# Modulation weights in the residual's place, a new order of projections, the router on unnormalised tokens, and the first gather ahead of later weights

## The chip, the cores and the metric

One core of a Trainium2 chip runs the whole kernel in one launch. Its engines are TensorE (PE; its weight loads are listed apart as PEld), VectorE (DVE), ScalarE (ACT) and GpSimd (POOL); SyncE (SP) only issues transfers. The metric is the device time of one execution in microseconds. A change of 0.2% (1.9 us) or more can be told from none for this kernel.

## The reference

One layer of a diffusion backbone in float32, width 1024, for 512 latent tokens (4 tiles of 128) and 128 context tokens (tile 4). Each kind has its own modulation vector.

```python
mod = silu(c) @ w_mod + b_mod                      # shift1, scale1, gate1, shift2, scale2, gate2
h = rmsnorm(x, g_norm1) * (1 + scale1) + shift1
p = h @ w_in        # xb, xc, xv (512 each), q, k (256 each), v, og (512 each), a_low (32)
y_a = xb * (conv3(xc * xv) + b_conv)               # along grid rows of 64, or the context
la = log_sigmoid(a_low @ w_a_up + b_a) / 16        # decay per direction, 4 heads
y_b = per_head_rmsnorm(gla_bidirectional(q, k, v, la)) * silu(og)
x = x + gate1 * (concat(y_a, y_b) @ w_out)
h = rmsnorm(x, g_norm2) * (1 + scale2) + shift2
probs = softmax(h @ w_router)                      # 16 experts; each takes its top 64 latent
gates, idx = top_k(probs.T, cap)                   # and top 16 context tokens
x = x + gate2 * scatter_add(gates * (silu(xs @ w_gate) * (xs @ w_up)) @ w_down)
y = rmsnorm(x, g_final)
```

The outputs are y for both kinds of tokens and the two final scan states of the context.

## The kernel before

The kernel has two phases. Phase one runs everything up to the choice of tokens, in an order written out by hand for each engine; phase two loops over 16 experts.

**Phase one.** TensorE's work is a list of jobs (`first_phase_jobs`, line 101). Each job ends with one step of the semaphore `job_done`, and each writes one of four pairs of PSUM banks. `place_jobs` gives a job the pair whose last job ended longest ago, except where `FORCED` names one; before a job TensorE waits in `claim` until the pair's previous job has been read (`read_by`). `HELD` keeps a pair until a later job, `LATE` lists jobs whose order of claims differs from that of their ends. The large projections work on two roundings: a weight part and a token part are split into a high half (ScalarE, `split_hi`, line 716; tokens `tokens_hi`) and a low half (VectorE, `split_lo`, line 1118), and each product is three passes, high-high, high-low, low-high (`passes`, line 1671). The modulated tokens stand in `hT`; their low half is written over them. The low-rank product for the decays (`low_rank`, line 1691) uses full float32 matmuls on the high and the low half, one after the other. A float32 matmul shows as two records, one of the rounded form as one.

Jobs have short names: `mod5` is the product with 512 columns of `w_mod`, `modT5` its turn to columns (`mod_turn`), after which VectorE's `modulation(5)` adds the bias; `xc0` to `xc3` are four parts of a projection (`project`), `v0` to `v4` the values by token tile (`values`), `la0` a head's log-decay, `ks0` a head's turned keys, `kv` key-value products, `att`, `o`, `oT` attention, head outputs and their turn, `g1` and `g2` rows of the gates, `wo0` to `wo4` the output projection by token tile, `x2T` the turned tile for the router, `lg` the router's product, `pT` and `pTc` turned scores, `ixT`, `ixTc`, `pcT` turned choices.

Weights of phase one come in units of 2 MB. `UNITS` is the order in which SyncE asks for them (`load_unit`, line 432), `PLACES` the buffer of each; a unit waits until the previous unit of its buffer has been used. SyncE handles its list strictly in order, so a wait in it holds back everything behind. Modulation units share buffers 0 and 1 with the projections' weights. The two cached states and later the residual `x_sb` are loaded into the region at `A_X`, which holds the input tokens until they are normalised.

**Output projection and router.** `output_projection(t, half)` (line 1887) makes 512 columns of tile t: 8 rows of 3 matmuls. VectorE's loop over tiles (from line 1418) reads each half from PSUM, multiplies by gate1, adds the residual, waits for the root of the mean square from ScalarE (`second_norm`), forms the inverse (`inverse_of`, four short steps) and writes normalised rows `xr` (`normalise`). ScalarE stores these rows to `hn` and the residual to `sum_l` in memory (`store_rows`, line 928). TensorE turns the normalised rows (`x2T`), ScalarE and VectorE copy four chunks each with scale2 and shift2 applied (`h2_turn`, `high_chunks`), and `router(t)` multiplies by `w_router_sb`. After the fourth tile VectorE takes the softmax and finds the top 64 for each expert in eight rounds. The context tile goes through GpSimd (line 587) meanwhile. In TensorE's order the dummy matmuls (`keep_warm`), the wait for the normalised context rows and their turn stand ahead of the turn of the latent choice (`turn_indices("ixT", 1)`).

**Phase two.** The first gather (`gather_first`, line 602) fetches 64 latent rows from `hn`. ScalarE modulates the turned rows, and each expert runs gate and up products for latent (line 2023) and context rows (2040), then down products (2063, 2072). Two turns for gate2's rows stand within expert 0. Expert weights pass through a ring of nine 2 MB slots, six loads per expert. Loads 0 to 2 are issued when the last head is gated; loads 3 to 8 each wait for a named event, load 9 and on for their slot.

## Time and profile before

| | us |
|---|---|
| time, median of 3 runs (935.05 to 936.36) | 935.1 |
| the profiled execution's own time | 934.86 |
| its span | 933.1 |
| TensorE busy | 876.1 |
| VectorE busy | 286.6 |
| ScalarE busy | 229.1 |
| GpSimd busy | 86.2 |
| moved between memory and the core | 273.33 MB, mean 293 GB/s |

Phase one lasts until 373.8 us, when the first expert matmul starts. The page's strip of forty slices shows TensorE busy nearly everywhere but in the first and last slices and near 350 to 375 us. A row of the chain of waits is a start, a length and what ran; a row of a timeline is a start, a length, the engine, the line and operation with its operands, and in brackets how long the engine had been idle and who released it. "Issue" is time without a visible wait.

### The profile page before, as it was taken

Reading aid. Unit: us, or ns where it says so; the run is one execution under the profiler, and the core shown is the slowest. Engines: PE = TensorE matmul, PEld = TensorE weight load, DVE = VectorE, ACT = ScalarE, POOL = GpSimd, SP = SyncE. Lnnn points to the kernel's source line nnn. Section 1 sums busy time; section 2 is a strip of 40 time slices with the busy share of each in tenths; the row PEclk is TensorE's granted clock in tenths of the full one; section 3 lists DMA queues with packets and bytes.
Section 4 is the critical chain, followed back from the end, with each engine's and each line's share of the span. In section 5 each row is a group of like instructions: output and inputs, shape, how many; then the busy total and the mean of one; then the engine's idle time right before and its main releaser. Section 6 shows DMA issues by size and latency. Waiting matters only on the chain.

```text
span 933.1 us, 14292 instructions
## 1 busy us (share of the span) xinstructions
PE 876.1 (94%) x6267; PEld 494.4 (53%) x6267; DVE 286.6 (31%) x589; ACT 229.1 (25%) x449; POOL 86.2 (9%) x87
## 2 busy tenths in 40 slices
PE   5798999999999995999999999999999999999994
PEld 4587889889897885333333333333333333333331
DVE  3455443668545645211011011101101101101215
ACT  5457343453224322211011011101101101101132
POOL 1000000000000012110110110011011011011013
PEclk9899999999999998999999999999999999999997
DMA  8914454552329239699999999999999999999973
GB/s 325 308 38 164 143 176 152 190 182 91 103 113 359 105 130 370 212 354 392 380 389 402 380 380 409 380 378 403 385 379 395 394 379 389 400 381 392 410 280 126
DMA packets 86180, 273.33 MB, mean 293 GB/s; under 512 B 6068, under 2 KB 9112, under 8 KB 86120
## 3 DMA queue, kind: packets, MB, share of 16 engines
q1 hardware_dynamic: 78376, 255.15, 71.3%
q0 software_dynamic: 6128, 11.87, 5.6%
q10 hardware_dynamic: 1616, 5.42, 1.5%
q8 instruction: 49, 0.80, 0.4%
q14 instruction: 11, 0.09, 0.0%
HBM read 257.94 MB, written 14.55 MB: 292 GB/s over the span
## 4 chain that ended last, share of the span: by engine, by line
PE 80%; DMA 7%; DVE 5%; ACT 4%; issue 2%; SPq 1%; POOL 1%; POOLq 0%; ACTq 0%; DVEq 0%
PE pair L2023 24%; PE pair L2040 12%; PE pair L1686 12%; PE pair L2063 11%; PE pair L2072 6%; PE pair L1897 5%; DMA p1w<-in_w_mod 4%; DMA p1w<-in_w_in 2%; PE pair L1722 2%; PE pair L1650 2%; DVE aT L1546 1%; DVE act_c L1544 1%; DMA p1w<-in_w_out 1%; ACT act_c L1009 1%; PE pair L1910 1%
## 5 line engine op out<-in xcount | busy, mean ns | idle before, releaser
L2023 PE MATMUL pair<-ring,xT 128*64 128x512 f32 x1024 | 225.3, 596 | 0.2 <-ACT xT L983 0.2
L2023 PEld LDWEIGHTS pair<-ring,xT 128*64 128x64 f32 x1024 | 72.2, 137 | 142.4 <-issue 142.3
L2063 PE MATMUL pair<-ring,aT 128*64 128x512 f32 x512 | 113.4, 595 | 1.1
L2040 PE MATMUL pair<-ring,xT 128*32 128x512 f32 x1024 | 113.2, 594 | 0.9 <-DVE xT L1533 0.9
L1005 ACT ACTIVATE act_l<-pair 128x512 f32<-128x512 f32 x16 | 9.6, 597 | 347.9 <-PE pair L2023 347.9
L1686 PE MATMUL pair<-hT_hi,w_hi 128*128 128x320 f32 x320 | 75.7, 318 | 5.8 <-DVE w_lo L1126 5.8
L1542 DVE TENSOR_TENSOR act_l<-act_l,pair 128x512 f32<-128x512 f32 x16 | 11.0, 687 | 207.8 <-ACT act_l L1005 207.8
L2040 PEld LDWEIGHTS pair<-ring,xT 128*32 128x32 f32 x1024 | 32.0, 110 | 79.7 <-issue 79.7
L1686 PE MATMUL pair<-hT_hi,w_lo 128*128 128x320 f32 x320 | 73.5, 311 | 0.0
L1686 PE MATMUL pair<-hT_lo,w_hi 128*128 128x320 f32 x320 | 73.4, 311 | 0.0
L2063 PEld LDWEIGHTS pair<-ring,aT 128*64 128x64 f32 x512 | 35.3, 137 | 68.8 <-issue 64.0
L625 POOL DMA_INDIRECT sum_l<-y_l,row_l x15 | 23.5, 1569 | 403.8 <-DVE y_l L1537 403.8
L1686 PEld LDWEIGHTS pair<-hT_hi,w_hi 128*128 128x128 f32 x320 | 53.5, 190 | 12.5 <-issue 11.6
L2072 PE MATMUL pair<-ring,aTc 128*32 128x256 f32 x1024 | 58.9, 381 | 0.0
L1686 PEld LDWEIGHTS pair<-hT_lo,w_hi 128*128 128x128 f32 x320 | 54.0, 189 | 0.0
L1686 PEld LDWEIGHTS pair<-hT_hi,w_lo 128*128 128x128 f32 x320 | 54.0, 190 | 0.0
L2072 PEld LDWEIGHTS pair<-ring,aTc 128*32 128x32 f32 x1024 | 31.5, 110 | 32.1 <-issue 13.0
L1544 DVE TENSOR_TENSOR act_c<-act_c,pair 64x512 f32<-64x512 f32 x16 | 11.0, 690 | 102.2 <-ACT act_c L1009 102.2
L1126 DVE TENSOR_TENSOR w_lo<-p1w,w_hi 128x1024 fp32r<-128x1024 f32 x24 | 29.0, 1223 | 42.0 <-ACT w_hi L726 41.8
L991 ACT ACTIVATE xT<-pair,mod,scale 128x64 f32<-128x64 f32 x120 | 37.1, 415 | 7.9 <-PE pair L1982 7.9
L1537 DVE SCALAR_TENSOR_TENSOR y_l<-pair,gain,gate_l 128x512 f32<-128x512 f32 x16 | 12.0, 750 | 74.8 <-PE pair L2063 74.8
L1897 PE MATMUL pair<-wo_hi,yT_hi 128*128 128x512 f32 x80 | 32.3, 404 | 1.4 <-DVE yT_lo L1360 1.4
(283 smaller groups left out, 972.4 us busy)
## 6 DMA issues: line engine op xcount, KB each, us to landing
...
```

Of the source, the lines that this page charges most:

```text
L625: g.indirect_dma_start(rows_l, bass.IndirectOffsetOnAxis(ap=row_l[:, e:e + 1], axis=0), y_l[:, e % 2, :], None, compute_op=ALU.add).then_i ...
L991: ins = a.activation(xT[:, k % 2, kk, 0:CAP_L], xT_ps(kk)[:, 0:CAP_L], ACT.Identity, bias=mod[:, 3 * KC + kk, 0:1], scale=scale2[:, kk, 0:1])
L1126: v.tensor_tensor(w_lo[place][:, :, tile(j)], p1w[place][:, :, tile(j)], rounded(name)[:, :, tile(j)].bitcast(F32), ALU.subtract).then_inc ...
L1544: v.tensor_tensor(act_c[0:64, :], act_c[64:P, :], ctx_ps[64:P, :], ALU.mult).then_inc(act_c_ready, 1)
L1650: ins = mm(pp[g:g + 32, 0:512], silu_c[:, k, :], w[:, k, :], start=k < 4, stop=k >= 4)
L1686: ins = mm(pp[:, s * 512:s * 512 + HALF], w, h[:, s * HALF:(s + 1) * HALF], start=k == 0 and i == 0, stop=k == KC - 1 and i == 2)
L1722: ins = mm(pp[:, cols], h, w, start=k == 0 and i == 0, stop=k == KC - 1 and i == 2)
L1897: ins = mm(pp[:, half * 512:(half + 1) * 512], y, w, start=k == 0 and i == 0, stop=k == KC - 1 and i == 2)
L2023: ins = mm(ps[64 * n:64 * n + 64, :], xt[:, kk, 0:CAP_L], w[:, j, n * 512:(n + 1) * 512], start=kk == 0, stop=kk == KC - 1)
L2040: ins = mm(ctx_ps[32 * g:32 * g + 32, :], xt[:, kk, CAP_L:96], w[:, j, n * 512:(n + 1) * 512], start=kk == 0, stop=kk == KC - 1)
L2063: ins = mm(y_ps[0][r:r + 64, :], aT[:, j, 64 * fh:64 * fh + 64], wd[:, j, n * 512:(n + 1) * 512], start=fh == 0 and j == 0, stop=fh == 1 a ...
L2072: ins = mm(y_ps[1][32 * b:32 * b + 32, 0:256], aTc[:, j, 32 * fh:32 * fh + 32], down[fh][:, j, 256 * b:256 * b + 256], start=fh == 0 and j ...
```

## The change

It has five parts.

1. A seventh buffer for phase-one weights, `p1w6`, lies at `A_X`. Five modulation units go through it (4, 5, 10, 6 and 11; 9, 7 and 8 keep buffers 0 and 1), and `UNITS` has a new order. The states are loaded after `mod11` has been used. `wo1` is asked for ahead of the residual.
2. The tokens before splitting move from `hT` to two buffers `raw`, which aren't overwritten, so `low_rank` reads them in one float32 pass.
3. The orders of jobs change on all engines: `la1` behind `v1`, `mod5` ahead of the key turns, `mod8` behind the attention products, `xb3` ahead of `o3`, `oT4` behind the first half of `wo0`, and others.
4. The router works on unnormalised tokens. `x2T` turns `x_sb`; the copies no longer modulate; the router's weights are scaled once by scale2 (`w_scaled`); the product of shift2 with the router is made once (`rb`), copied by VectorE (`shifted`), spread over 128 rows on TensorE (`rbT`), and added when VectorE reads the logits, together with the factor 1/rms. Normalised rows are still made, for `hn`.
5. At the end of phase one gate2's rows are turned directly after the context's output projection, there are fewer dummy matmuls, load 5 of the ring waits for the first gather's landing, and ScalarE issues the copies of the context's residual to `sum_c` after `first_tokens`; load 7 waits for them as before.

```diff
+    jobs += ["mod1", "mod3", "modT1", "modT3", "q0", "q1", "k0", "alow", "k1", "la0"]
+    jobs += ["v0", "v1", "la1", "mod4", "v2", "mod9", "v3", "v4", "mod5", "ks0", "ks1", "modT4", "modT9", "la2"]
+    jobs += ["xc0", "xc1", "modT5", "xc2", "mod10", "xc3", "ks2", "modT10"]
+    jobs += ["xv0", "la3", "xv1", "mod6", "xv2", "modT6", "xv3", "mod11", "ks3"]
+    jobs += ["og0", "modT11", "mod7", "kv0", "kv1", "og1", "kv2", "kv3", "og2", "modT7", "kv4", "og3"]
+    jobs += ["xb0", "att0", "att1", "mod8", "xb1", "modT8", "o0", "att2", "o1", "oT0", "att3", "xb2"]
+    jobs += ["oT1", "o2", "att4", "xb3", "o3", "oT2", "o4", "oT3", "g1_0", "g1_1", "rb", "oT4"]
+    jobs += ["rbT", "wo0", "wo1", "x2T0", "x2T1", "lg0", "wo2", "lg1", "x2T2", "wo3", "lg2", "x2T3", "lg3", "pT", "wo4", "g2_0", "g2_1", "x2T4", "ixT", "lg4", "pTc", "ixTc", "pcT"]
...
-LATE = ["wo0", "wo1", "wo2", "x2T0", "lg0", "x2T1", "wo3", "lg1", "x2T2", "wo4", "x2T3", "lg2", "lg3", "pT"]
-HELD = {"q0": "modT3", "q1": "modT3", "k0": "modT3", "wo4": "pT"}
-FORCED = {"x2T4": 1, "ixT": 0, "lg4": 3, "pTc": 1, "ixTc": 3, "pcT": 1, "g2_0": 3, "g2_1": 1}
+LATE = ["wo0", "oT4", "rbT", "wo1", "x2T0", "wo2", "x2T1", "lg0", "lg1", "wo3", "x2T2", "lg2", "wo4", "x2T3", "lg3", "pT"]
+HELD = {"q0": "modT3", "q1": "modT3", "k0": "modT3", "mod5": "la2", "wo4": "pT"}
+FORCED = {"g2_0": 2, "g2_1": 1, "x2T4": 2, "ixT": 0, "lg4": 3, "pTc": 1, "ixTc": 3, "pcT": 1}
...
-UNITS = ["mod0", "mod2", "qk", "mod1", "mod3", "v", "mod4", "mod9", "xc", "mod5", "mod10", "xv", "mod6", "mod11", "og",
+UNITS = ["mod0", "mod2", "qk", "mod1", "mod3", "v", "mod4", "mod9", "mod5", "xc", "xv", "mod10", "mod6", "og", "mod11",
  "mod7", "xb", "mod8", "wo0", "wo1"]
-PLACES = [2, 5, 0, 1, 4, 1, 0, 0, 0, 1, 1, 1, 0, 0, 0, 1, 1, 0, 0, 1]
+PLACES = [2, 5, 0, 1, 4, 1, 6, 0, 6, 0, 1, 6, 6, 0, 6, 1, 1, 0, 0, 1]
...
+p1w.append(at("p1w6", A_X, [P, KC, 512]))
...
+w_scaled = at("w_scaled", R_V + 4096, [P, KC, 2, E])
...
-    for n in range(UNITS.index("v"), UNITS.index("og")):
-        load_unit(n)
+    load_unit(UNITS.index("v"))
     sp.wait_ge(ss_ready, NT)
     sp.wait_ge(xr_ready, NT)
+    for n in range(UNITS.index("mod4"), UNITS.index("xb")):
+        load_unit(n)
+    sp.wait_ge(job_done, job("mod11") + 1)
     sp.dma_start(states[0:DK, 0, :, :], s_fwd[0, 0].rearrange("h d v -> d h v")).then_inc(st_in, 16)
     sp.dma_start(states[DK:P, NCH_LAT - 1, :, :], s_bwd[0, 0].rearrange("h d v -> d h v")).then_inc(st_in, 16)
-    for n in range(UNITS.index("og"), UNITS.index("wo1")):
+    for n in range(UNITS.index("xb"), UNITS.index("wo1")):
         load_unit(n)
     sp.wait_ge(fin_state, 1)
     sp.dma_start(new_f[0, 0].rearrange("h d v -> d h v"), final_state[0:DK, :, :]).then_inc(state_out, 16)
     sp.dma_start(new_b[0, 0].rearrange("h d v -> d h v"), final_state[DK:P, :, :]).then_inc(state_out, 16)
+    load_unit(UNITS.index("wo1"))
     sp.wait_ge(job_done, job("o4") + 1)
     for t in range(NT):
         src = x_sample[0, tile(t), :] if t < NT - 1 else x_prompt[0]
         sp.dma_start(x_sb[:, t, :], src).then_inc(x_in[t], 16)
-    load_unit(UNITS.index("wo1"))
...
     load_rows(3)
     sp.wait_ge(job_done, job("wo4") + 1)
     load_rows(4)
+    sp.wait_ge(xs_full[0], 16)
     load_rows(5)
...
     split_hi("wo0", 0)
...
     o_square(0)
     o_square(1)
     split_hi("wo0", 2)
-    for t in range(2, NT):
-        o_square(t)
+    o_square(2)
     split_hi("wo0", 3)
+    o_square(3)
     mixed_hi(0)
     mixed_hi(1)
+    o_square(4)
     gate_row("g1_0", 0, gate1b, g1_ready)
     gate_row("g1_1", 1, gate1b, g1_ready)
...
+        rows = slice(KC // 2 * half, KC // 2 * half + KC // 2)
+        a.activation(h2T[t % 2][:, rows, :], pp[:, 512 * half:512 * half + 512].rearrange("p (k n) -> p k n", n=P),
+                     ACT.Copy).then_inc((h2_low, h2_high)[half], 1)
     for t in range(NT - 1):
-        if 1 <= t < NT - 2:
-            h2_turn(t - 1)
+        second_norm(t)
         if t + 2 < NT:
             mixed_hi(t + 2)
-        second_norm(t)
-        if t == NT - 2:
-            h2_turn(t - 1)
         store_rows(t)
-    h2_turn(NT - 2)
+        h2_turn(t)
...
     ctx_half(0)
     ctx_half(1)
+    for v in range(2):
+        gate_row(f"g2_{v}", v, gate2b, g2_ready)
     act.wait_ge(x2c_ready, 2)
     square_sum(NT - 1)
+    h2_turn(NT - 1)
+    h2_turn(NT - 1, 1)
     act.wait_ge(rootc_ready, 1)
     a.activation(xr[:, 0, :], x_sb[:, NT - 1, :], ACT.Copy, scale=rms[:, 5, NT - 1:NT]).then_inc(xrc_ready, 1)
-    h2_turn(NT - 1)
-    h2_turn(NT - 1, 1)
+    act.wait_ge(xrc_ready, 1)
     act.dma_start(hn[tile(NT - 1), :], xr[:, 0, :]).then_inc(hn_out[0], 16)
-    act.dma_start(sum_c[0:P, :], x_sb[:, NT - 1, :]).then_inc(sums_in, 16)
-    act.dma_start(sum_c[P:P + PAD, :], x_sb[0:PAD, NT - 1, :]).then_inc(sums_in, 16)
...
     first_tokens()
-    for v in range(2):
-        gate_row(f"g2_{v}", v, gate2b, g2_ready)
+    act.dma_start(sum_c[0:P, :], x_sb[:, NT - 1, :]).then_inc(sums_in, 16)
+    act.dma_start(sum_c[P:P + PAD, :], x_sb[0:PAD, NT - 1, :]).then_inc(sums_in, 16)
...
     split_lo("wo0", 2)
+    head_norm(2)
     att_mask(4)
-    head_norm(2)
+    gated_conv(3)
+    split_lo("wo0", 3)
     gated(2)
     head_norm(3)
+    mixed_lo(0)
+    mixed_lo(1)
     gated(3)
     head_norm(4)
-    gated_conv(3)
-    split_lo("wo0", 3)
-    mixed_lo(0)
     gated(4)
-    mixed_lo(1)
     for j in range(4):
         split_lo("wo1", j)
     dve.wait_ge(g1_ready, 2)
+    dve.wait_ge(job_done, job("oT4") + 1)
+    dve.wait_ge(scale_ready, 3)
+    dve.wait_ge(decay_in, 144)
+    for i in range(2):
+        ins = v.tensor_tensor(w_scaled[:, :, i, :], w_router_sb[:, :, :],
+                              scale2[:, :, i:i + 1].to_broadcast([P, KC, E]), ALU.mult)
+    ins.then_inc(wscaled_ready, 1)
+    pp = result(dve, "rb")
+    v.tensor_copy(shifted[:, :], pp[0:2, 0:E]).then_inc(rb_ready, 1)
     def high_chunks(t):
         pp = result(dve, f"x2T{t}")
         if t >= 2:
             dve.wait_ge(job_done, job(f"lg{t - 2}") + 1)
-        for k in range(KC // 2, KC):
-            ins = v.tensor_scalar(h2T[t % 2][:, k, :], pp[:, k * P:(k + 1) * P],
-                                  scale2[:, k, vec(t):vec(t) + 1], mod[:, 3 * KC + k, vec(t):vec(t) + 1],
-                                  ALU.mult, ALU.add)
-        ins.then_inc(h2_high, 1)
+        v.tensor_copy(h2T[t % 2][:, KC // 2:, :], pp[:, 512:1024].rearrange("p (k n) -> p k n", n=P)
+                      ).then_inc(h2_high, 1)
     def router_row(t):
         pp = result(dve, f"lg{t}")
-        v.tensor_copy(logits[:, t, :], pp[:, 0:E]).then_inc(lg_ready, 1)
-    dve.wait_ge(scale_ready, 3)
+        v.scalar_tensor_tensor(out=logits[:, t, :], in0=pp[:, 0:E], scalar=rms[:, 5, t:t + 1],
+                               in1=shift_rows[:, vec(t), :], op0=ALU.mult, op1=ALU.add).then_inc(lg_ready, 1)
     for t in range(NT - 1):
+        pp = pairs[PAIR[f"wo{t}"]]
+        dve.wait_ge(x_in[t], 32)
         if t >= 2:
             dve.wait_ge(hn_out[t % 2], 16 * (t // 2))
-            dve.wait_ge(job_done, job(f"x2T{t - 2}") + 1)
-        pp = pairs[PAIR[f"wo{t}"]]
-        dve.wait_ge(x_in[t], 32)
         for half in range(2):
             cols = slice(512 * half, 512 * half + 512)
             dve.wait_ge(*((wo_half, t + 1) if half == 0 else (job_done, job(f"wo{t}") + 1)))
...
                             ).then_inc(wo_read, 1)
             dve.wait_ge(wo_read, 2 * t + half + 1)
             v.tensor_tensor(x_sb[:, t, cols], x_sb[:, t, cols], xr[:, t % 2, cols], ALU.add).then_inc(x2_ready, 1)
-        if 1 <= t < NT - 1:
-            high_chunks(t - 1)
+        if t == 0:
+            pp = result(dve, "rbT")
+            v.tensor_copy(shift_rows[:, :, :], pp[:, 0:2 * E].rearrange("p (v e) -> p v e", v=2)
+                          ).then_inc(rbT_ready, 1)
         if t + 2 < NT:
             mixed_lo(t + 2)
+        if t == NT - 2:
+            high_chunks(t)
         dve.wait_ge(root_ready, t + 2)
         inverse_of(rms, slice(t, t + 1), EPS)
         normalise(t)
-        if t >= 2:
-            router_row(t - 2)
-    high_chunks(NT - 2)
-    router_row(NT - 3)
+        if t < NT - 2:
+            high_chunks(t)
+        if t:
+            router_row(t - 1)
     router_row(NT - 2)
     def softmax(lo, hi, turn):
...
+    def turn_tile(t):
+        pe.wait_ge(*((x2_ready, 2 * t + 2) if t < NT - 1 else (x2c_ready, 2)))
+        turn_rows(f"x2T{t}", NT, x_sb[:, t])
+    def shift_products():
+        pe.wait_ge(mod_ready, 10)
+        pe.wait_ge(decay_in, 144)
+        pp = claim(pe, "rb")
+        for k in range(KC):
+            ins = mm(pp[0:2, 0:E], mod[:, 3 * KC + k, :], w_router_sb[:, k, :], start=k == 0, stop=k == KC - 1)
+        end(ins, "rb")
+    def shift_spread():
+        pe.wait_ge(rb_ready, 1)
+        pp = claim(pe, "rbT")
+        for i in range(2):
+            ins = mm(pp[:, i * E:(i + 1) * E], ident[0:2, i:i + 1].to_broadcast([2, P]), shifted[:, :],
+                     start=True, stop=True)
+        end(ins, "rbT")
...
-                for i, h in enumerate((hT_hi, hT_lo)):
-                    ins = mm(pp[g:g + 32, s * 512:s * 512 + HALF], w_tail[:, k, :],
-                             h[:, k, tok].bitcast(F32), start=k < 4 and i == 0, stop=k >= 4 and i == 1)
+                ins = mm(pp[g:g + 32, s * 512:s * 512 + HALF], w_tail[:, k, :], tokens_raw(k)[:, tok],
...
     log_decay(0)
-    log_decay(1)
     values(0)
     values(1)
+    log_decay(1)
     mod_products(4)
     values(2)
     mod_products(9)
     values(3)
     values(4)
+    mod_products(5)
     turn_ks(0)
     turn_ks(1)
     mod_turn(4)
...
     project("xb0", "xb", 0)
-    mod_products(8)
     attention(0)
     attention(1)
+    mod_products(8)
     project("xb1", "xb", 1)
     mod_turn(8)
     pe.wait_ge(state_step, 2 * NCH_LAT)
...
     turn_heads(1)
     head_outputs(2)
     attention(4)
+    project("xb3", "xb", 3)
     head_outputs(3)
     turn_heads(2)
     pe.wait_ge(state_step, 2 * NCH_LAT + 2)
     head_outputs(4)
     turn_heads(3)
-    project("xb3", "xb", 3)
-    turn_heads(4)
     pe.wait_ge(mod_ready, 7)
     gate_rows(1, 2 * KC, 0)
     gate_rows(1, 2 * KC, 1)
...
         pe.wait_ge(h2_high, t + 1)
         pp = claim(pe, f"lg{t}")
         for k in range(KC):
...
+    shift_products()
     output_projection(0, 0)
+    turn_heads(4)
+    shift_spread()
     output_projection(1, 0)
     output_projection(0, 1)
     output_projection(1, 1)
+    turn_tile(0)
     output_projection(2, 0)
-    turn_rows("x2T0", NT + 1, xr[:, 0])
+    turn_tile(1)
+    pe.wait_ge(wscaled_ready, 1)
+    router(0)
     output_projection(2, 1)
-    router(0)
-    turn_rows("x2T1", NT + 2, xr[:, 1])
+    router(1)
     output_projection(3, 0)
-    router(1)
+    turn_tile(2)
     output_projection(3, 1)
-    turn_rows("x2T2", NT + 3, xr[:, 0])
-    output_projection(4, 0, range(5))
-    turn_rows("x2T3", NT + 4, xr[:, 1])
     router(2)
+    output_projection(4, 0, range(1))
+    turn_tile(3)
+    output_projection(4, 0, range(1, 2))
     router(3)
-    output_projection(4, 0, range(5, KC))
+    output_projection(4, 0, range(2, KC))
     def turn_probs(name, turns, tiles):
         pe.wait_ge(probs_ready, turns)
...
             mm(pp[:, 0:P], ident[:, :], ident[:, :], start=True, stop=True)
...
     output_projection(4, 1)
-    keep_warm("x2T4", 6)
-    pe.wait_ge(xrc_ready, 1)
-    turn_rows("x2T4", NT + 4, xr[:, 0])
+    pe.wait_ge(mod_ready, 12)
+    gate_rows(2, 5 * KC, 0)
+    gate_rows(2, 5 * KC, 1)
+    keep_warm("x2T4", 4)
+    turn_tile(4)
     keep_warm("ixT", 8)
     turn_indices("ixT", 1)
     router(4)
-    pe.wait_ge(mod_ready, 12)
     keep_warm("pTc", 8)
     turn_probs("pTc", 2, (NT - 1,))
-    keep_warm("ixTc", 8)
+    keep_warm("ixTc", 3)
```

## Rows read from the trace of the kernel before

**Rows 1.** Busy time by stretch, in the loop: engines, granted clock, DMA share, GB/s.
```profile
400.00:500.00 100.00, 98.95 (x716) 36.17 (x712) 12.94 (x24) 10.98 (x30) 12.28 (x9) 1.00 1.03 389
```
**Rows 2.** TensorE's waits, whole span: total us, times, longest.
```profile
PE pair L1665 <- ACT xr L970: 6.5, 1, 6.5
...
PE pair L1650 <- DMA p1w<-in_w_mod: 4.8, 5, 1.2
```
**Rows 3.** Timelines of ScalarE, VectorE and TensorE around the third values tile.
```profile
87.09 1.06 ACT L792 ACTIVATE v_sb<-pair 128x512 f32<-128x512 f32 x2
...
89.77 0.89 DVE L1174 TENSOR_SCALAR work_a<-pair,param 128x640 f32<-128x640 f32 x1 [0.99 <-ACT work_b L772]
...
90.75 0.56 PE L1722 MATMUL pair<-w_hi,hT_hi 128*128 128x256 f32 x1 [3.52 <-issue]
```
**Rows 4.** The chain of waits from 59 to 118 us: start, length, what.
```profile
59.98 4.51 PE pair L1700 x64
...
90.75 8.40 PE pair L1722 x48
...
101.00 11.72 PE pair L1722 x96
...
117.29 7.04 PE pair L1686 x48
```
**Rows 5.** Busy time by stretch, four stretches of phase one.
```profile
31.30:34.70 3.40, 3.31 (x12) 3.34 (x13) 3.39 (x4) 3.40 (x6) 0.00 (x0) 0.50 1.04 386
...
90.70:93.00 2.30, 2.25 (x10) 2.28 (x11) 0.33 (x1) 2.27 (x3) 0.00 (x0) 0.50 1.05 408
...
117.30:187.70 70.40, 68.40 (x479) 61.28 (x478) 35.38 (x49) 30.99 (x42) 1.85 (x2) 1.00 0.49 168
...
342.20:345.00 2.80, 2.80 (x8) 1.92 (x8) 0.79 (x4) 0.26 (x1) 0.00 (x0) 0.50 0.00 0
```
**Rows 6.** Timeline of SyncE: the issue of the first state transfer.
```profile
162.58 0.67 SPq L472 DMA_DIRECT2D states<-in_state_gla_fwd  x1
```
**Rows 7.** The chain of waits from 186 to 319 us.
```profile
186.91 9.10 DMA p1w<-in_w_mod
...
235.21 9.54 DMA p1w<-in_w_out
244.78 1.06 ACT wo_hi L726
...
252.14 0.66 PE pair L1839 x4
...
283.10 27.50 PE pair L1897 x120
...
316.96 1.69 PE pair L1910 x16
```
**Rows 8.** Timeline of VectorE from 280 to 360 us.
```profile
282.96 0.69 DVE L1354 TENSOR_TENSOR yT<-pair,og_sb 128x512 f32<-128x512 f32 x1
...
288.60 4.63 DVE L1126 TENSOR_TENSOR w_lo<-p1w,wo_hi 128x1024 fp32r<-128x1024 f32 x4 [3.82 <-ACT wo_hi L726]
...
346.11 0.41 DVE L1459 COPY probs_half<-pair 48x256 f32<-48x256 f32 x1 [2.73 <-PE pair L1939]
...
358.54 0.21 DVE L1484 TENSOR_TENSOR selr<-merge 16x64 f32<-16x64 f32 x1
```
**Rows 9.** Timeline of TensorE: turn of the choice, first expert matmuls.
```profile
363.77 0.23 PE L1945 MATMUL pair<-ident,selr 16*128 16x16 f32 x1
...
373.79 4.80 PE L2023 MATMUL pair<-ring,xT 128*64 128x512 f32 x16 [0.16 <-ACT xT L983]
```
**Rows 10.** The first three gathers (372.5, then free engines), issue to landing.
```profile
DMA to landing us min/median/max: 2.9/3.9/8.0
```
**Rows 11.** The chain of waits, last expert's latent gate and up products.
```profile
885.52 13.88 PE pair L2023 x64
```
**Rows 12.** The ring load issued at 869.3 us, issue to landing.
```profile
DMA to landing us min/median/max: 18.4/18.4/18.4
```

96 lines of the change are left out of this document (44 added, 52 removed).

## The prediction

> **What bounds the kernel now.** I read the busy time by stretch first, then TensorE's waits, then the chain of waits and the timelines around each wait. From 400 to 500 us TensorE is busy 98.95 of 100 us, and the rest of the expert loop is the same [rows 1]; so the loop ends in TensorE, and what an edit is worth is read in the stages ahead of it. There the reader should see a few waits: 6.5 us for the context's normalised rows, 4.8 over five waits for modulation weights [rows 2], 3.5 at the values' projection [rows 3]. One more limit is hidden: transfers run at a share of 1.03 in the loop [rows 1], so it is close to being bound by them as well; that is the slower rival below. I work in stages and carry the time of one event to the next.
>
> **Stage A, to the first conv projection (117.3 us now).** The low-rank product takes 4.51 us for 64 records [rows 4]; it drops one of two passes, 32 records: -2.25. The wait of 3.52 us is the third values tile: its bank held log-decay 1, whose last reader ran on VectorE until 90.66 (89.77 + 0.89) [rows 3]. With log-decay 1 issued two tiles later, the bank is the first values tile's, read by ScalarE until 87.7 (half of the two copies from 87.09) [rows 3], in the new run 85.5. TensorE comes there at about 84.5, so a wait of 1 us stays. The chain shows the wait's second price: the tile behind it took 8.40, where two tiles take 11.72 [rows 4], at a granted clock of 0.50, the 1.2 GHz level [rows 5]. That is 2.5 us more, which a wait of 1 us should not cost (the waits of 1.0 to 1.2 for weights are in stretches of full clock, as the row of stage B). Values end at 105.0 (85.5 + 5.9 + 1.9 + 11.7) instead of 112.7. The product moved to here costs 1.9; the turns and log-decay 2 follow as before, without the wait of 1.3 among them, since two weight parts are now rounded ahead of the last values copy. First conv projection at 109.6, 7.7 earlier.
>
> **Stage B, to the first output-gate projection (187.7 now).** The stretch holds 70.4 us, 68.4 of them busy [rows 5]. The 2.0 of waits for weights go, because modulation weights have a place of their own and are asked for a projection or more ahead; one product (1.9, paid in A) and one turn (0.4, paid in C) go as well. 66.1 stay, and 0.4 for later bank releases: 176.1, 11.6 earlier.
>
> **Stage C, to the first output-projection matmul (283.1 now).** Here the change adds waits. The weights of modulation 7 are asked for only behind the end of product 11 and the issues of two state transfers, 0.67 each [rows 6]; that load now takes 9.10 [rows 7], so it lands 10.5 behind product 11. TensorE has 8.1 us of work in between: a wait of 2.4 instead of 1.2, and 0.4 for the turn, +1.6. The wait of 1.0 for modulation 8 goes (attention now stands ahead of it), but its product ends 1 us later behind the last output-gate projection, and there the load of the output weights starts. It takes 9.54, and the first head was turned 7.4 us behind its landing (252.14 - 244.78), ScalarE and VectorE being queued behind the splits [rows 7]. TensorE arrives 1 us earlier, the rows 0.9 later: a wait of 2.3 for 0.4. Behind that the wait of 1.4 and a head turn (0.4) leave; the shift products come, 16 narrow records, between 0 and a router's 1.69 [rows 7], of which I take 0.9, nearer the middle since their weights are narrow; and 1.6 of waiting for the last head's norm, which VectorE now reaches behind two splits of 1.2. Sum: 274.6, 8.5 earlier.
>
> **Stage D, to the copy of the turned scores (346.1 now).** Here I expect most of the gain to be lost. The new row spread on TensorE waits for a small copy of the shift on VectorE. In VectorE's order that copy stands behind the last gated head, which needs the head turn behind the first half projection, then behind four splits of the second half's weights, then behind two scaled copies of the router. With the first matmul at T: turn done T+5.9 (24 of 120 records in 27.5 [rows 7], and 0.4), gated head T+6.7 (0.69), splits T+11.3 (4.63) [rows 8], small copies T+12. TensorE stands for 6.1 us, and the whole output projection is queued behind it. At the start of the kernel the clock was 0.50 for 3.4 us after such a gap, in the values' row 2.5 us were lost [rows 4, 5]; I add 2. With turn and spread (0.6) the last latent projection ends 8.75 later than now counted from T. From there to the copy it is now 13.8 us. The transposes no longer wait for a norm, but ScalarE copies tile 3's transpose only after it has stored the normalised rows: residual, router 2, one row of the context projection and transpose 3.3 us, then VectorE's copy, inverse and norm 2.2, two issues and a copy on ScalarE 1.4, so router 3 at 6.95 and done at 8.6. Six rows of the context projection then stand ahead of the scores' turn, 18 records of 0.23, and 1.6 for a clock that fell behind two routers now as well (0.50 from 342.2) [rows 5]: 15.2 in all, +1.4. Score copy at 274.6 + 63.0 + 10.2 = 347.8: the gain has turned into 1.7 of loss. The plain copies for modulated ones are shorter and lie beside projections; I count nothing for them. Without that cover each tile would be 0.8 shorter.
>
> **Stage E, to the first expert matmul (373.8 now).** It takes 27.7 from the score copy. The latent choice is ready at 358.75, its turn comes at 363.77, behind the context's norm and transpose on TensorE: 5.0 us lost [rows 8, 9]. The context's transpose now needs only the residual, so the choice is turned at 358.8. The gather starts 0.7 behind the turn and landed 8.0 after its start, with three weight loads ahead; the two gathers that met free engines took 2.9 and 3.9 [rows 10]. With one load ahead, which has landed by then, I take 3.9: 363.4. Router 4, dummy matmuls and the turn of its scores keep TensorE until 363.5, so the first matmul is at 364.4 in the old time, 18.3 behind the copy; 366.1 in the new. The Trainium skill (DMA: Bandwidth & Descriptors, "Queues, rings and completion order") says that each DMA engine takes turns, packet by packet, between the queues it has work for. A gather would then be slowed by loads on another queue, but not wait for their end, and holding one load back would give little. The 8.0 us beside 3.9 speaks against that here; the result is rival 3.
>
> **Stage F, the first expert.** Two gate-row turns leave it, 1.0 each, and fill idle time of stage E: -2.0. Its first 16 records took 4.80 us, where 16 take 3.5 in the loop (64 in 13.88) [rows 9, 11]; with TensorE kept busy I count 0.9. From there the loop repeats. Total 7.7 + 2.0 + 0.9 = 10.6 us. The profiled execution took 934.86 us, 1.8 of it around the span of 933.1, and 0.2 below the median of 935.1: 924.3.
>
> **Rivals.** (1) VectorE has the shift ready in time: 8 us more come through, 916. For it: nothing in the two orders; against: 4.63 and 0.69 are rows. (2) The waits of 2.4, 2.3 and at router 3 let the clock fall too, 2 to 2.5 us behind each: 930. For it: it fell behind 3.52; against: it did not behind 1.2. (3) Holding back a load gives nothing, since the gather shares the engines in any case and takes 8 again: 4.4 more, 929. For it: what stands in E on queues; against: 3.9. (4) The slower one, in the loop: weights come late. Now the tightest load starts at 869.3, lands 18.4 later at 887.7 [rows 12] and is used half way through the gate and up products, 885.52 + 7 = 892.5 [rows 11]: a lead of 4.8. Loads 5 and 6 now start 10 us later than before, and load 7 only after the copies to the sums, which stand behind the first tokens on ScalarE. I expect load 7 at 377 and load 9 landed at 395, 10 us earlier than now, as TensorE is: the lead stays near 4. It decides from 394 for load 7: then load 9 lands over 4.8 later than now and every further microsecond is lost whole beside the gain; with 397 it is 938. For it: the share of 1.03; against: 17 us of room.
>
> **How the numbers follow.** Forecast 0.60 (own range 920 to 929), rival 1 0.10, rival 2 0.15, rival 3 0.08, rival 4 0.07. The time is the forecast's. Its bounds: 0.9 either way for the shift products, 2 for the clock in D, 1 for bank releases. The range 917 to 931 adds rivals 2 and 3 and stops short of most of 1. A change under 0.2% (1.9 us) can't be told from none. Slower is rival 4: 0.07; same is 0.04, taken from rivals 2 and 3 where they fall together (935); faster is the rest, 0.89.
>
> **What would show it.** Right: no wait over 1.5 us at the values, the first conv projection near 110, the first output gate near 176, a wait near 2.4 for modulation 7, one TensorE wait of about 6 us released by VectorE's small copy, 6 us behind the first output-projection matmul, the score copy near 348, the first gather landed within 4.5 us, no wait for weights in the loop. Without the 6 us wait, or with the score copy before 342, the sum is wrong and rival 1 right; with waits for ring slots near the end rival 4 is.

## The result and the profile after

| | us |
|---|---|
| kernel before, median of 6 runs | 935.22 (934.19 to 937.3) |
| kernel after, median of 6 runs | 930.05 (928.78 to 932.41) |
| ratio | 0.9944, 95% interval 0.9928 to 0.9959 |
| profiled execution of after, its span | 932.41, 930.6 |
| forecast | 924.3 (917 to 931) |

The kernel is 5.2 us faster (0.6%); forecast were 10.8. The sign held and the time lies inside the range, near its upper end; of the gain less than half came. The profiled execution is the slowest of the six, 2.4 above their median; the second profile of the same kernel below (e5) has 929.88.

Events in the two profiles, in us from the span's start (the chain of waits for the first two, timelines for the rest):

| event | before | forecast | after | gained: forecast, measured |
|---|---|---|---|---|
| A first conv projection | 117.3 | 109.6 | 111.5 | 7.7, 5.8 |
| B first output gate | 187.7 | 176.1 | 177.4 | 11.6, 10.3 |
| C first output projection | 283.1 | 274.6 | 271.9 | 8.5, 11.2 |
| D copy of turned scores | 346.1 | 347.8 | 350.3 | -1.7, -4.2 |
| E first expert matmul | 373.8 | 366.1 | 370.4 | 7.7, 3.4 |
| F expert 1's first matmul | 413.4 | 402.8 | 406.4 | 10.6, 6.9 |
| end of the span | 933.1 | 922.5 | 930.6 | 10.6, 2.5 |

So the stages ahead of the loop fell 3.7 short, and the loop and its tail gave back 4.4 where I had nothing.

The stretch of [rows 1] looks the same after: TensorE 98.93 of 100, DMA share 1.03.

```profile
400.00:500.00 100.00, 98.93 (x716) 36.01 (x714) 12.94 (x24) 11.00 (x30) 12.30 (x9) 1.00 1.03 388
```

TensorE's waits after (total, times, longest). The 6.5 of [rows 2] is gone, the five waits for modulation weights are two; the small copy's 5.8 stands where the forecast put it (6.1), and 3.3 at the router too. What answers to nothing in the forecast is the wait for ring weights, and the 2.5 within the first row.

```profile
PE pair L2093 <- DVE act_c L1564: 6.8, 16, 2.5
PE pair L1697 <- DVE shifted L1419: 5.8, 1, 5.8
PE pair L1948 <- ACT h2T L952: 3.3, 1, 3.3
PE pair L2065 <- DMA ring<-in_w_up: 2.7, 1, 2.7
PE pair L1690 <- DVE norm_r L1356: 1.7, 1, 1.7
PE pair L1670 <- DMA p1w<-in_w_mod: 1.3, 2, 1.1
```

The chain of waits after, stages A to C. Against [rows 4]: the low-rank product takes 2.29 instead of 4.51, and the tile behind the former wait 6.00 instead of 8.40. The product at 184.89 stands straight behind its turn: no wait for modulation 7.

```profile
61.08 2.29 PE pair L1739 x32
...
86.62 6.00 PE pair L1761 x48
...
111.52 8.50 PE pair L1726 x58
...
184.45 0.44 PE pair L1678 x4
184.89 1.85 PE pair L1670 x16
```

Timeline of VectorE after, ahead of the copy of the shift. These are the operations that the forecast queued ahead of it: gated head, four splits, two scaled copies, the copy at 285.18, on which TensorE starts at 285.39.

```profile
279.62 0.69 DVE L1363 TENSOR_TENSOR yT<-pair,og_sb 128x512 f32<-128x512 f32 x1 [8.45 <-PE pair L1877]
280.23 4.62 DVE L1134 TENSOR_TENSOR w_lo<-p1w,wo_hi 128x1024 fp32r<-128x1024 f32 x4
284.77 0.48 DVE L1415 TENSOR_TENSOR w_scaled<-w_router_sb,scale 128x128 f32<-128x128 f32 x2
285.18 0.15 DVE L1419 COPY shifted<-pair 2x16 f32<-2x16 f32 x1
```

Timeline of TensorE after, expert 13: half way through its gate and up products it stands 2.66 for weights.

```profile
811.11 7.09 PE L2065 MATMUL pair<-ring,xT 128*64 128x512 f32 x32
820.86 7.09 PE L2065 MATMUL pair<-ring,xT 128*64 128x512 f32 x32 [2.66 <-DMA ring<-in_w_up]
```

ScalarE and TensorE after, in the last expert. ScalarE has its squares of the sums ahead of the context's activation; the squares wait for a load, so TensorE waits for the activation. The chain that ended last now leads back to that load, 13.81 us long.

```profile
900.43 1.06 ACT L1008 ACTIVATE xs_square<-x_sb 128x1024 f32<-128x1024 f32 x1 [4.40 <-DMA x_sb<-sum_l]
```
```profile
905.47 0.66 PE L2093 MATMUL pair<-ident,act_c 128*128 128x128 f32 x4 [2.49 <-DVE act_c L1564]
```
```profile
889.09 13.81 DMA x_sb<-sum_l
```

### The profile page after: what moved, and what is told of

It reads as the page before. It is cut to its first block, busy times and chain, and to the rows that moved or that the text cites. A ratio compares the mean times of both kernels' runs of the same rounds, so it can differ in the third digit from the quotient of the medians.

```text
span 930.6 us, 14218 instructions
## 1 busy us (share of the span) xinstructions
PE 875.6 (94%) x6241; PEld 495.1 (53%) x6241; DVE 284.0 (31%) x581; ACT 224.2 (24%) x431; POOL 86.4 (9%) x87
## 4 chain that ended last, share of the span: by engine, by line
issue 39%; PE 32%; DMA 20%; DVE 5%; ACT 2%; SPq 1%; POOLq 0%; ACTq 0%; DVEq 0%
PE pair L1726 14%; DMA sum_l<-y_l,row_l 14%; PE pair L1935 6%; DMA p1w<-in_w_in 2%; PE pair L1761 2%; PE pair L1670 2%; PE pair L2065 2%; DMA x_sb<-sum_l 1%; PE pair L1948 1%; DMA p1w<-in_w_mod 1%; DMA p1w<-in_w_out 1%; PE pair L2105 1%; DVE w_lo L1134 1%; PE pair L2082 1%; DVE x_sb L1613 1%
## 5 line engine op out<-in xcount | busy, mean ns | idle before, releaser
L2105 PEld LDWEIGHTS pair<-ring,aT 128*64 128x64 f32 x512 | 35.3, 137 | 68.8 <-issue 64.0
L1935 PE MATMUL pair<-wo_hi,yT_hi 128*128 128x512 f32 x80 | 34.5, 431 | 0.0
## 6 DMA issues: line engine op xcount, KB each, us to landing
p1w<-in_w_mod SPq DMA_DIRECT2D x12, 2048.0 KB, 10.4
```

Source lines behind the costliest of these rows:

```text
L1935: ins = mm(pp[:, half * 512:(half + 1) * 512], y, w, start=k == 0 and i == 0, stop=k == KC - 1 and i == 2)
L2105: ins = mm(y_ps[0][r:r + 64, :], aT[:, j, 64 * fh:64 * fh + 64], wd[:, j, n * 512:(n + 1) * 512], start=fh == 0 and j == 0, stop=fh == 1 a ...
```

## The experiments

Each was timed beside runs of the kernel before on the same chip. There that kernel took 936.7 to 938.1 by median, so ratios are compared, not times. Below, "after" is the changed kernel, "loop" the time from expert 0's first matmul to the span's end: 559.3 before, 560.2 after.

### The wait for the small copy (e1)

```diff
             head_norm(4)
+            pp = result(dve, "rb")
+            v.tensor_copy(shifted[:, :], pp[0:2, 0:E]).then_inc(rb_ready, 1)
             gated(4)
...
             ins.then_inc(wscaled_ready, 1)
-            pp = result(dve, "rb")
-            v.tensor_copy(shifted[:, :], pp[0:2, 0:E]).then_inc(rb_ready, 1)
```

> VectorE copies the shift right behind the last head's norm, ahead of the last gated head and the four splits; nothing else changes. Theory (the 5.8 us wait of TensorE for this copy is a plain loss of stage D, and the loads 3 to 8, which are issued on events of TensorE, move with it): the wait of 5.8 goes, with 1.7 for the 72 slow records behind it, first expert matmul near 363, time 930 - 7 = 923. Rival (the wait is covered: from the first expert on the transfers set the end, and they do not move): 929 to 930.

Measured 924.33, ratio 0.9859 (0.9827 to 0.9891), against 0.9944. The wait is gone; the 72 records behind it take 16.6 us instead of 18.2, so 1.6 of the loss was the clock (the forecast took 2). The first expert matmul comes at 361.8, 8.6 ahead of after's first profile; the loop takes 560.6. Loads moved with TensorE, and the wait for weights moved along too (2.7, ending at 812.6). Here the clock fell behind it: the 32 records that followed took 8.78 us where they take 7.09 in after (mean granted clock 0.55 from 815.0 to 817.5). The theory holds.

One more thing is in this run. Behind the same wait of 1.73 and the same 16 narrow products, the first 24 records of the output projection took 5.75 here and 7.3 in after. The clock fell there and not here; over the 13 profiles of versions of after in this study it fell in nine (7.3) and held in four (5.75: e1, e5, e9, e10). So 1.6 of the 8.6 is not the edit's. Against e5, whose clock held too, the first expert matmul is 5.7 earlier, router 3 having cost 1.6 more here. By stretch, first after, then e1 (the column ahead of the last two is the granted clock; 0.50 is 1.2 GHz):

```profile
272.00:274.00 2.00, 2.00 (x7) 1.57 (x7) 0.00 (x0) 2.00 (x3) 0.00 (x0) 0.69 1.03 422
274.00:276.00 2.00, 2.00 (x6) 1.51 (x6) 0.00 (x0) 0.47 (x1) 0.00 (x0) 0.50 0.69 281
```
```profile
272.00:274.00 2.00, 2.00 (x10) 1.61 (x10) 0.00 (x0) 1.93 (x3) 0.00 (x0) 1.00 1.02 414
```

### The hold of load 5 (e2, e6)

e2 takes the hold away; e6 keeps it only until the gather is issued:

```diff
-            sp.wait_ge(xs_full[0], 16)
+            sp.wait_ge(first_issued, 1)      # e6; e2 has neither line
             load_rows(5)
...
+                g.memset(half_col[:, :], -0.5).then_inc(first_issued, 1)   # e6, GpSimd, behind the first gather
```

> Load 5 no longer waits for the first gather's landing, so loads 5 and 6 are issued at 356 and 360 instead of 368, ahead of the gather. Theory (the end hangs on transfers, which are never idle from 370 on): the gather lands 3.5 later (8.0 for 4.5), TensorE's first expert starts 3 later, but the stream has two loads' time more behind it; the wait of 2.7 for weights near 820 goes and the end is the same within 1.5, 929 to 931. Rival (TensorE sets the end): 3 to 4 slower, 933 to 934.

> Load 5 is held until the first gather is issued, by a small write of GpSimd behind it, not until it has landed: 3.5 us earlier (364.9 for 368.3 on the first run's clock). Theory (in step E a gather is delayed by what was issued ahead of it, in step F on the end is set by transfers): gather still 4.5 to 5, first expert matmul unmoved within 1, the stream 3 us ahead, end 2 to 3 less than the changed kernel. Rival (a gather shares the engines with loads issued behind it too): gather 7 to 8, first expert matmul 3 later, end unchanged.

e2: ratio 0.9951 (0.9931 to 0.9971), the same as after. The gather took 9.1 instead of 4.5, the first expert matmul came 3.9 later and its first 16 records took 5.79 for 3.65, so TensorE lost 6.0 by the context products; then no wait for weights, and all but 1.7 of it was back at the end. A microsecond lost on TensorE ahead of the loop is not one at the end here. e6: 0.9903 (0.9874 to 0.9932), 3.5 better than e5 beside it. The gather took 5.9, the first expert matmul stayed at 370.6, the loop took 557.6 without a wait for weights. Both went as the theory had it, but for the gather in e6, whose 5.9 lies between the theory's 4.5 to 5 and the rival's 7 to 8: a load issued behind a gather slows it somewhat. The first gather's landing (issue to landing) in after, e6 and e2:

```profile
DMA to landing us min/median/max: 4.5/4.5/4.5
```
```profile
DMA to landing us min/median/max: 5.9/5.9/5.9
```
```profile
DMA to landing us min/median/max: 9.1/9.1/9.1
```

### One load shortened (e3 after, e4 before)

```diff
-sp.dma_start(ring[n % TURNS][:, :, :], src...)
+blocks = 1 if n == 34 else 4
+sp.dma_start(ring[n % TURNS][:, 0:blocks, :], src...[:, 0:blocks, :])
```

> One of the 96 ring loads (expert 5, first down half) brings one block of 128 rows instead of four, 1.5 MB less, about 4 us of transfers; that expert's products use what the buffer held, so the output differs. Theory (the loop of the changed kernel is bound by transfers): no wait for weights near 820, sums land 3 to 4 earlier, time 926 to 928, 2 to 4 less. Rival (TensorE sets the end): 930, no change.

> The same shortened load in the kernel before. Theory (that kernel is bound by TensorE, with transfers 1 to 5 us ahead of it): 935, change under 1. Rival (it is bound by transfers just as well): 931 to 932.

e3: ratio 0.9926 (0.99 to 0.9952). No wait for weights, loop 557.6 for 560.2; the sums are still waited for 3.6. The ratio is 0.0016 to 0.0018 under that of after, 1.5 to 1.7 us: less than the theory's 2 to 4, and not told from none. e4: 1.0008 (0.9987 to 1.0028), nothing, and its loop takes 559.8. So fewer bytes take 2.6 us off the changed kernel's loop and none off the one before; that is read from the profiles, not from the times.

### The changed kernel again (e5)

No edit.

> The changed kernel unaltered, beside the others of this call, since its first profiled run held a wait of 2.7 us for weights that is not certain to be in every run. Theory (bound by transfers from the first expert on): the wait near 820 is there again, and the end lies 560 to 561 us behind the first expert matmul. Rival (one chance delay in one run): no such wait, and the end 558 us behind it. Ratio to the kernel before near 0.994 in both.

930.82, ratio 0.9942 (0.9919 to 0.9966). The wait is there again (2.1), the loop takes 560.6, the wait for the sums 4.9. Expert 1 starts at 403.6, 9.8 ahead of before's profile, and the span ends 5.0 ahead: the loss is no accident of one run.

### The turn of tile 3 (e7)

```diff
+                if t == NT - 2:
+                    h2_turn(t)
                 store_rows(t)
-                h2_turn(t)
+                if t < NT - 2:
+                    h2_turn(t)
```

> ScalarE copies tile 3's transpose for the router ahead of the two stores of that tile instead of behind them. Theory (the wait of 3.3 us at router 3 and the slow clock behind it are a plain loss of stage D): the wait is 0.5 to 1, router 3 takes 1.8 instead of 2.8 and the 18 records behind it 4.3 instead of 6.6, score copy and end 4 to 5 earlier. Rival (the clock falls all the same, or the gather then waits for the later stores): 2 or less.

925.54, ratio 0.9877 (0.9845 to 0.9908): 5 to 6 less than e5, the theory's 4 to 5 or a little more. The router starts 0.1 behind the row ahead of it, the 18 records behind it take 4.4 for 6.75. The score copy comes at 344.1; from there to the first expert matmul it takes 21.7 instead of 20.1, slow records again, so a part went back. There is no wait for weights (loop 558.6). Router 3, after and then e7:

```profile
340.08 2.79 PE L1948 MATMUL pair<-w_scaled,h2T 128*128 128x16 f32 x16 [3.28 <-ACT h2T L952]
```
```profile
337.20 1.93 PE L1951 MATMUL pair<-w_scaled,h2T 128*128 128x16 f32 x16
```

### The part for the first gather, in the kernel before (e8, e13, e14)

e8 turns the choice first, e13 has the hold alone, e14 both:

```diff
+            turn_indices("ixT", 1)
             pe.wait_ge(xrc_ready, 1)
             turn_rows("x2T4", NT + 4, xr[:, 0])
-            keep_warm("ixT", 8)
-            turn_indices("ixT", 1)
+            keep_warm("lg4", 8)
...
             load_rows(4)
+            sp.wait_ge(xs_full[0], 16)
             load_rows(5)
```

> The kernel before with one thing changed: TensorE turns the latent choice ahead of the context's rows instead of behind them; the first gather is issued 5 us earlier (359.5 for 364.5), the loads ahead of it are not held. Theory of step E (a gather lands only with the loads ahead of it, the last of which is issued at 355.1 and landed at 374.4): it lands at 370 to 372 as before, 10 to 12 after its issue, gain 0 to 2, so that the new order is worth little without the hold. Rival (it shares the engines and takes 8 from its issue): lands at 367.5, first expert matmul 3 to 5 earlier.

> The kernel before with the hold alone: load 5 waits for the first gather's landing. Theory (the hold takes the gather from 8.0 to 4.5 and lets TensorE start the context products 5 to 6 earlier, and pays for it with a stream of loads that starts later, so that the end is bound by transfers): first expert matmul 3 to 4 earlier, a wait for ring weights or for the sums' loads in the loop's end, time only 1 to 3 less, 934 to 936 where the kernel before has 937. Rival (the price of the stream is special to the changed kernel): the whole 5 to 6 less, 931, no wait for weights.

> The kernel before with the choice turned ahead of the context's rows and the hold: the part of the change that was meant for step E, alone. Theory: gather issued 4 us earlier and landed after 4.5 instead of 8, first expert matmul bound by the dummy products, 4 to 5 earlier; loads 5 and 6 issued at 365; end 559 to 560.5 behind the first expert matmul, ratio 0.995 to 0.997, that is, this part brings 3 to 4 of the changed kernel's 5. Rival (as in step E of the forecast): 7 to 9 earlier at the first expert matmul and as much at the end, ratio 0.991.

e8: 0.997 (0.9951 to 0.999). The gather issued at 360.6 took 7.9 and landed at 368.5, 4 ahead of before, though loads 4 to 6 were ahead of it: the rival's landing, not mine. The Trainium skill (DMA: Bandwidth & Descriptors, "Queues, rings and completion order") has a DMA engine take turns between queues by packets; the trace agrees here, since load 6, issued 4.5 us ahead of the gather, landed at 375.7, 7 behind it. The first expert matmul gained only 2.3 from the score copy on (25.4 for 27.7), since dummy products stood ahead until 371.5.

e13: 0.9978 (0.9962 to 0.9993). The gather took 4.1, but the first expert matmul comes 27.05 behind the score copy: the dummies again, ahead of the rows' turn (timeline of TensorE; 32 records at 0.50 to full clock, 5.6 us). There is no wait for weights in its loop. So the time came out as the theory had it (0.9978 is 2.1 less) and the mechanism didn't: the first expert matmul gained 0.6 and not 3 to 4, and the hold alone doesn't make the stream short. e14: 0.9982 (0.9962 to 1.0003), not told from e8 or e13, nor from no change; its gather took 3.9, its first expert matmul came 25.6 behind the score copy, its loop has no wait for weights either. In the kernel before, order and hold are worth 3 us at most, not the 9 of step E.

```profile
369.70 3.37 PE L1963 MATMUL pair<-ident 128*128 128x128 f32 x16
373.08 2.19 PE L1963 MATMUL pair<-ident 128*128 128x128 f32 x16
375.19 0.71 PE L1987 MATMUL pair<-ident,xs 64*128 64x64 f32 x8
```

### The load order that I had read (e9)

```diff
-            for n in range(UNITS.index("mod4"), UNITS.index("xb")):
+            for n in range(UNITS.index("mod4"), UNITS.index("mod7")):
...
-            for n in range(UNITS.index("xb"), UNITS.index("wo1")):
+            for n in range(UNITS.index("mod7"), UNITS.index("wo1")):
```

> The load order that the prediction read into the change, made true: the weights of modulation 7 are asked for behind the end of product 11 and the two state transfers, not a projection ahead of them. Theory (step C's error was a misreading of the loop of loads, its sum was right for the order it assumed): TensorE waits 2 to 2.5 at product 7, the first output-projection matmul is 2.5 to 3.5 later, and so is the end. Rival (the wait is hidden by attention or by the load of the output weights): under 1.5.

Ratio 0.9942 (0.9921 to 0.9964), the same as after. The wait appears, 1.71, and the first output-projection matmul is 1.4 later, counted from the low-rank product. So the order was misread, and the sum for the order assumed was too dear by about half: 1.4 is under the rival's 1.5, not the theory's 2.5 to 3.5, and the end shows none of it.

```profile
185.63 1.92 PE L1670 MATMUL pair<-p1w,silu_c 128*32 128x512 f32 x16 [1.71 <-DMA p1w<-in_w_mod]
```

### The tail (e10)

```diff
+            def sums_home():   # ScalarE, ahead of the last expert; SyncE's loop is gone
+                act.wait_ge(d_used, 2 * (E - 1))
+                act.wait_ge(yl_added, 16 * (E - 1))
+                for t in range(NT - 1):
+                    act.dma_start(x_sb[:, t, :], sum_l[tile(t), :]).then_inc(sums_back[t], 16)
+                act.wait_ge(yc_added, 16 * (E - 1))
+                act.dma_start(x_sb[:, NT - 1, :], sum_c[0:P, :]).then_inc(sums_back[NT - 1], 16)
```

> The five last loads of the sums are issued by ScalarE on its own queue, not by SyncE behind the last two down loads. Theory (the tail of the changed kernel hangs on these loads, which land 3.8 behind the last ring load, and that one is needed only when the down product starts 7 us later): they land 4 to 7 us after issue instead of 12 to 14, ScalarE's wait of 4.4 and TensorE's of 2.5 go, end 1.5 to 3 earlier than the changed kernel. Rival (they share the engines and land as late, or delay the last down load into its product): no change, or a wait at the last down product.

Ratio 0.9942 (0.9917 to 0.9968): no change. The loads took 11 by median and the last 15.7; TensorE's 2.5 went, but the end still hangs on the last of them: from the context products of the last expert to the end it took 36.6, where after took 35.3 and e5 35.8. The rival holds.

```profile
886.87 15.71 DMA x_sb<-sum_c
```

### The copies of the context's sums (e15)

```diff
             act.dma_start(hn[tile(NT - 1), :], xr[:, 0, :]).then_inc(hn_out[0], 16)
+            act.dma_start(sum_c[0:P, :], x_sb[:, NT - 1, :]).then_inc(sums_in, 16)
+            act.dma_start(sum_c[P:P + PAD, :], x_sb[0:PAD, NT - 1, :]).then_inc(sums_in, 16)
...
             first_tokens()
-            act.dma_start(sum_c[0:P, :], x_sb[:, NT - 1, :]).then_inc(sums_in, 16)
-            act.dma_start(sum_c[P:P + PAD, :], x_sb[0:PAD, NT - 1, :]).then_inc(sums_in, 16)
```

> The two copies to the context's sums are issued ahead of the first tokens again, as in the kernel before, 5.5 us earlier (364.5 for 370.1), and load 7, which waits for them, with them. Theory (what decides is the time from the issue of load 5, where the gapless stream begins, to expert 1's first matmul: 38.1 us with a wait for weights of 2.1 to 2.7, 41.9 without; work taken out of the stream counts the same): 1.7 us of copies leave the stream, the gather is at most 1 later, the wait for weights shrinks to 0 to 1, end 0.5 to 2 less than the changed kernel, ratio 0.992. Rival (rival 4 of the forecast, the late load 7 itself is what is short, issued 8.7 behind the first expert matmul): no wait for weights and the sums' loads land 3 to 4 earlier, 3 to 4 less, ratio 0.990.

929.48, ratio 0.9914 (0.9886 to 0.9941). Load 7 went out at 369.3 instead of 379.0, the wait for weights is gone and the loop takes 557.0 for 560.2. So a piece of the change's own fifth part cost about 3 us of the loop. Half of the gain was paid for ahead of the loop: the gather takes 5.2 instead of 4.5 here, and from the score copy to the first expert matmul it is 21.6 for 20.1. In time the gain over after (0.0028, 2.6 us) isn't clear of the intervals. Theory and rival can't be told apart by the time either; the sums are still waited for 4.2, against the rival, which had their loads 3 to 4 earlier.

### Together (e11, e12, e16)

e11 is e1, e6 and e7 in one kernel; e12 adds e10 and 5 dummies for 8; e16 is e11 with e15.

> The edits of three earlier runs together: shift copied early, tile 3 turned before its stores, load 5 held only until the gather is issued. Theory (each takes away a loss on TensorE ahead of the first expert or a gap of the transfers, and loads move with TensorE): they add up, 7 + 5 + 3 = 15 less than the changed kernel, ratio to the kernel before 0.978 to 0.980. Rival (the transfers' end is fixed by something that does not move): they share one gain, ratio 0.985 or more.

> The three edits, the sums' loads on ScalarE's queue, and 5 dummy products (10 records) instead of 8 (16) ahead of the context scores' turn, which at the lower clock stood 1.6 us past the moment that the scores were ready. Theory: 2 to 3 less than the run with three edits for the tail, 0 to 1 for the dummies; ratio 0.975 to 0.978, 913 to 916. Rival (the tail gains nothing): as the run with three edits.

> The three edits that added up to 914.0 (shift early, tile 3 turned before its stores, load 5 held to the gather's issue) and the context's sum copies ahead of the first tokens. Theory: TensorE's start as there or 1 later, stream 1.7 shorter, so 0 to 1.5 less, ratio 0.972. Rival (the copies delay the gather, on which the first expert waits in that kernel): 1 to 2 more, ratio 0.974 to 0.975.

e11: 914.0 (912.33 to 915.38), ratio 0.9732 (0.9698 to 0.9765), the best version: 2.7% below before, where after is 0.6% below. Against e5 the ratio falls by 0.0210, where the three alone take off 0.0083, 0.0039 and 0.0065, 0.0187 together: they add up within the intervals. The score copy is at 335.7 instead of 350.3, and no wait for weights is left in the loop (557.4). e12: 0.9742 (0.971 to 0.9773) and e16: 0.9754 (0.9719 to 0.9789), neither told from e11. The dummies' edit brings nothing, since the gather is what the first expert waits for (20.5 behind the score copy in both); the tail's doesn't either (36.3 from the last expert's context products on, 35.4 in e11). e15's edit brings nothing either; that the stream has room already would explain it, but isn't shown.

## Why the prediction was right or wrong

Two steps failed and were dear: the clock in stage D (3.1 of the stage's 5.2 us), and "From there the loop repeats" in stage F, with rival 4's "the lead stays near 4" behind it (4.4). Stage C, with its misread order of loads, was 4.0 too dark and hid that much of their cost. That the time lies inside the range is owed in part to this luck.

**Stage A** (1.9 short). The wait, its clock price and the halved product came out as worked out. But 1.1 is there before the changed code is reached: the low-rank product starts at 61.1 instead of 60.0, and in the other runs anywhere from 59.7 to 61.8, in both kernels. The stage's end was one profile's accident to that extent. Another 0.6 is a slip in my sum: from the end of the values, 112.7, to the conv projection, 117.3, it was 4.6, and without the wait of 1.3 that leaves 3.3, where 105.0, 1.9 and 109.6 leave 2.7; measured 3.5.

**Stage B** held: 65.9 for 66.5.

**Stage C** (4.0 too dark). The step "The weights of modulation 7 are asked for only behind the end of product 11 and the issues of two state transfers" is a misreading. The first loop of loads runs up to `xb` and includes modulation 7, whose buffer waits only for `xv`'s last part. Its end is at 167.4; the load was there when TensorE came at 184.9, without the wait of 2.4 that I had. e9 shows what my order really costs, 1.4. The rest is the wait for the first output head, 0.84 instead of 2.3, the load of the output weights having taken 7.95 instead of 9.54. Two terms were right: 1.73 at the last head's norm (1.6), 0.55 for the shift products (0.9).

**Stage D** (5.2 short). Its mechanism is shown by e1: wait, operations and order as forecast. What failed above all is the term for the clock. I charged it once, 2 us behind the 6 us wait, and once at the routers. It fell three times: 1.6 behind the wait of 1.73, where I had counted nothing; 1.6 behind the long one; and behind the 3.3 us wait at router 3 the router took 1.1 more than 1.69, and the 18 records 2.4 more than their 4.4 at full clock, 3.5 together where I had 1.6. That is 3.1 more than I had. The last head's turn and the spread of the shift took 1.5 together for 0.6. And one turn was overlooked: tile 2's now stands ahead of the last row of the latent projection, which it stood behind in the kernel before, another 0.9:

```profile
326.38 0.87 PE pair L1705 x8
```

e7 gave the 3.5 back. Rival 2 named the clock, and its 930 is the time that was measured, but by chance: two of the waits that it names (2.4 and 2.3) were 0 and 0.8 long, and the loss in the loop, which it doesn't have, made up for them.

**Stage E** (7.6 gained where 9.4 was forecast). The turn of the choice came when it was ready, and the held gather took 4.5 (I took 3.9). But the dummy products, 16 records in 3.6 us at the fallen clock, kept the scores' turn until 368.5, and TensorE's turn of the rows stood behind it and six more records until 369.3, with the gather landed at 368.2. For rival 3: a gather does share the engines with loads in flight (7.9 from its issue in e8, 9.1 in e2), yet with load 4 landed and only a store of 0.5 MB beside it, it took 4.5, so the hold worked.

**Stage F** gained 3.5, forecast 2.9.

**The loop and the tail** (4.4, not in the forecast; rival 4 had 0.07). The rival's mechanism came true and its threshold was wrong by far: it was to decide from 394 for load 7, and load 7 went out at 379, near the 377 that I expected. The lead of 4.8 at the last expert [rows 12] is what is left of a larger one. Here is the same load of an expert (the first up half), issue to landing, in the kernel before, issued at 430.9, 599.5 and 734.4:

```profile
DMA to landing us min/median/max: 9.3/9.3/9.3
```
```profile
DMA to landing us min/median/max: 12.6/12.6/12.6
```
```profile
DMA to landing us min/median/max: 15.7/15.7/15.7
```

With 18.4 at 869.3, that is 9.1 in 13 experts: the stream falls back by 0.7 us per expert against TensorE. After, the load issued at 457.8 already took 14.4, the one at 761.2 took 22.3:

```profile
DMA to landing us min/median/max: 14.4/14.4/14.4
```
```profile
DMA to landing us min/median/max: 22.3/22.3/22.3
```

It is needed some 23 us behind its issue (892.5 less 869.3), so one expert later it came late. So the loop needs about 9 us of lead when it begins (an estimate, 13 times 0.7). In the kernel before, the queues were empty just then (DMA share by stretch, before and then after; last two columns share and GB/s):

```profile
390.00:395.00 5.00, 4.13 (x34) 1.65 (x34) 2.74 (x8) 1.44 (x2) 0.90 (x1) 1.00 0.04 15
```
```profile
390.00:395.00 5.00, 4.83 (x48) 2.16 (x40) 0.63 (x1) 0.72 (x2) 0.00 (x0) 1.00 1.03 354
```

The landing of load 9, the first that waits for a used buffer, tells the lead at the loop's start. It took 7.6 before and in e2, 10.4 to 10.9 in e11, e12, e15 and e16, all without a wait for weights; 13.2 in e9, which waited 1.1 and 0.2, 13.4 in e10, which waited 2.1, and 14.2 in e1, which waited 2.7. Before, then e1:

```profile
DMA to landing us min/median/max: 7.6/7.6/7.6
```
```profile
DMA to landing us min/median/max: 14.2/14.2/14.2
```

So the rival's yardstick, a load 9 over 4.8 later against TensorE, agrees with every one of these runs (7.6 and 4.8 are 12.4); only e3, whose load was shortened, had 13.4 and no wait. What failed is the step from load 7 to load 9: "load 9 landed at 395" is its issue and the old 7.6. It left out that loads 5 to 8, the copies and the gathers now all stand close ahead of it, and that costs it 6 us more. The share of 1.03 that I had read was the warning, and I priced it only by when one load starts.

The 4.4 can be split by the context products of the first and the last expert, before and then after:

```profile
393.53 7.07 PE L2040 MATMUL pair<-ring,xT 128*32 128x512 f32 x64 [0.87 <-DVE xT L1533]
899.34 7.07 PE L2040 MATMUL pair<-ring,xT 128*32 128x512 f32 x64
```
```profile
386.62 7.07 PE L2082 MATMUL pair<-ring,xT 128*32 128x512 f32 x64 [0.87 <-DVE xT L1553]
895.32 7.07 PE L2082 MATMUL pair<-ring,xT 128*32 128x512 f32 x64
```

Between them before took 505.8, and so did all other profiles without a wait for weights (e7 506.3); after took 508.7, e5 508.5, and e1, with the slow records behind its wait, 510.6. From the last one to the end before took 33.8, after 35.3, e5 35.8 and e7 36.1. So 2.7 to 2.9 of the loss is the wait for weights, 1.5 to 2.0 the tail, where the loads of the sums queue behind the last ring loads. In e2, without the hold, both are gone (505.8 and 33.9). In e1 the slow records cost nothing in the end: its tail is shorter instead (33.7), and from the first context products to the end it took 544.3, as e5 did. That fits transfers setting the end. How to take away the tail's part at no cost ahead of the loop I have not found; e10 didn't.

What stays open: why the clock falls behind the wait of 1.73 in some runs and not in others, and what spreads the kernel before over 933 to 941 in these runs.
